# Half rows of the output projection put between the levels of the RWKV inverse

## The reference, cut to what matters

```
z = _rmsnorm(h, mix_pre_g[l]) @ w_in[l]
y_att = _attention_group(z[..., :ATT_IN], cos, sin, attn_out_g[l])
y_rwkv = _rwkv7_group(z[..., ATT_IN:], ...)      # a scan over the tokens, in both directions
mix = jnp.concatenate([y_att, y_rwkv], axis=-1) @ w_out[l]
h = h + _rmsnorm(mix, mix_post_g[l])
f = _swiglu(_rmsnorm(h, ffn2_pre_g[l]), ffn2_w_gate[l], ffn2_w_up[l], ffn2_w_down[l])
```

## Time and profile before

| what | us |
|---|---|
| median of 3 runs | 1143.54 |
| profiled execution | 1142.37 |
| span of the profiled execution | 1140.6 |
| TensorE busy | 1123.6 |
| GpSimd busy | 917.1 |
| ScalarE busy | 633.9 |
| VectorE busy | 542.2 |

### The profile page before, as it was taken

How to read it: one execution, slowest core, us unless ns; L and a number is a source line. 1 busy time by engine, 2 the same in 40 slices (tenths; PEclk the granted TensorE clock), 3 DMA queues, 4 the chain that set the end, 5 groups by cost and what they waited for, 6 DMA issues and landing times.

```text
span 1140.6 us, 24340 instructions
## 1 busy us (share of the span) xinstructions
PE 1123.6 (99%) x10090; PEld 1048.1 (92%) x10090; DVE 542.2 (48%) x1006; ACT 633.9 (56%) x1024; POOL 917.1 (80%) x709
## 2 busy tenths in 40 slices
PE   9999999999999999999999999999999799999998
PEld 9998999999998999999999999999988679999997
DVE  5542575642653223222644333467986466233333
ACT  6666675447644654444744444588664437444443
POOL 6997667875996999989799999698785036999994
PEclk9999999999999999999999999999999999999999
DMA  7655445555565665565556565565610035556563
GB/s 287 194 168 183 129 131 166 204 164 151 185 222 184 211 190 187 189 185 185 166 185 187 186 186 187 193 201 165 199 55 23 4 113 186 186 186 187 188 188 101
DMA packets 54302, 193.50 MB, mean 170 GB/s; under 512 B 6448, under 2 KB 7344, under 8 KB 53808
## 3 DMA queue, kind: packets, MB, share of 16 engines
q1 hardware_dynamic: 52464, 185.41, 51.2%
q10 hardware_dynamic: 1728, 6.53, 1.5%
HBM read 188.77 MB, written 1.05 MB: 166 GB/s over the span
## 4 chain that ended last, share of the span: by engine, by line
PE 95%; DVE 2%; POOL 1%; issue 1%; ACT 1%; DMA 0%; DVEq 0%; POOLq 0%; ACTq 0%
PE product L635 19%; PE product L637 19%; PE product L636 19%; PE bank L765 8%; PE bank L767 7%; PE bank L766 7%; PE product L1382 2%; PE bank L1337 1%; PE bank L1331 1%; PE product L864 1%; PE product L1331 1%; PE product L793 1%; PE product L865 1%; PE product L866 1%; PE bank L822 1%
## 5 line engine op out<-in xcount | busy, mean ns | idle before, releaser
L583 POOL TENSOR_TENSOR weight_lo<-raw_ring,weight_hi 128x512 fp32r<-128x512 f32 x684 | 892.1, 1337 | 191.3 <-ACT weight_hi L2772 177.7
L2772 ACT ACTIVATE weight_hi<-raw_ring 128x1024 fp32r<-128x1024 f32 x338 | 356.7, 1059 | 362.6 <-DMA raw_ring<-in_ffn_gu 108.6
L635 PE MATMUL product<-operand_B_hi,weight_hi 128*128 128x256 f32 x1104 | 312.0, 283 | 0.2 <-POOL weight_lo L583 0.2
L637 PE MATMUL product<-operand_B_hi,weight_lo 128*128 128x256 f32 x1104 | 310.9, 282 | 0.0
L636 PE MATMUL product<-operand_B_lo,weight_hi 128*128 128x256 f32 x1104 | 310.5, 281 | 0.0
L635 PEld LDWEIGHTS product<-operand_B_hi,weight_hi 128*128 128x128 f32 x1104 | 207.8, 188 | 3.3 <-POOL weight_lo L583 0.4
L636 PEld LDWEIGHTS product<-operand_B_lo,weight_hi 128*128 128x128 f32 x1104 | 207.9, 188 | 3.1
L637 PEld LDWEIGHTS product<-operand_B_hi,weight_lo 128*128 128x128 f32 x1104 | 207.8, 188 | 0.0
L635 PE MATMUL product<-operand_A_hi,weight_hi 128*128 128x256 f32 x712 | 203.8, 286 | 0.1
L636 PE MATMUL product<-operand_A_lo,weight_hi 128*128 128x256 f32 x712 | 200.4, 282 | 0.0
L637 PE MATMUL product<-operand_A_hi,weight_lo 128*128 128x256 f32 x712 | 200.4, 281 | 0.0
(11 more groups left out here) (436 smaller groups left out, 1538.6 us busy)
## 6 DMA issues: line engine op xcount, KB each, us to landing
raw_ring<-in_w_in SPq DMA_DIRECT2D x95, 512.0 KB, 3.6
raw_ring<-in_ffn_gu SPq DMA_DIRECT2D x88, 512.0 KB, 3.6
raw_ring<-in_ffn_down SPq DMA_DIRECT2D x44, 512.0 KB, 3.5
raw_ring<-in_w_mlp_up SPq DMA_DIRECT2D x32, 512.0 KB, 3.6
raw_ring<-in_w_mlp_down SPq DMA_DIRECT2D x32, 512.0 KB, 3.5
raw_ring<-in_w_out SPq DMA_DIRECT2D x14, 512.0 KB, 3.7
raw_ring<-in_w_gmlp_v SPq DMA_DIRECT2D x8, 512.0 KB, 3.5
raw_ring<-in_w_branch_c SPq DMA_DIRECT2D x8, 512.0 KB, 3.5
```

Source lines behind the costliest of these rows:

```text
L583: last = k.nc.gpsimd.tensor_tensor(k.wlo[:, slot, part], k.raw[:, slot, part], k.whi[:, slot, part].bitcast(F32), ALU.subtract)
L635: mm(ps, w_hi, op.hi[:, b, :], start=b == 0, stop=False)
L637: return mm(ps, w_lo, op.hi[:, b, :], start=False, stop=b == blocks - 1)
L2772: k.nc.scalar.activation(k.whi[:, slot, 0:w], k.raw[:, slot, 0:w], ACT.Copy).then_inc(k.s["hi_ready"], 1)
```

## The change

All eight pieces of the first token half of tiles 0 to 3 (half rows 0, 2, 4, 6) move between the levels, each behind a group of small products. For that the attention output is made earlier on all engines (`attention_by_feature` stands behind the second level and not the fourth), the banks of the levels of chunks 2 and 3 change so that banks 0 and 1 are free, and `values_first(1)` and `state_behind(1)` become `from_state(1)`. The half rows of the second token half (1, 3, 5, 7) go among the parts of chunk 3, and `last_outputs(3)` goes ahead of `feature_major(0)`. The number of products is the same. The core of the diff:

```diff
-    k.state_banks = (k.slots[1], k.chain_bank, k.slots[1])
-    k.left_banks, k.both_banks = (k.bank[1], k.slots[0]), (k.bank[0], k.bank[3])
+    k.state_banks = (k.chain_bank, k.chain_bank, k.slots[1])
+    k.left_banks = ((k.bank[1], k.slots[0]), (k.slots[1], k.slots[0]))
+    k.both_banks = ((k.bank[0], k.bank[3]), (k.bank[2], k.bank[3]))
-    k.turn_bank = [k.bank[2], k.slots[1]]
+    k.turn_bank = [k.bank[0], k.bank[1]]
...
-        pe.wait_ge(s["op_ready"], k.made["y_mix"].base + AB)
+        pe.wait_ge(s["u_ev"], nth(3, 5))
...
-    pe.wait_ge(s["z_ev"], 10)
-    chunk_products(3, 0, SPARE_BANKS)
+    pe.wait_ge(s["z_ev"], 12)
+    chunk_products(3, 0, LANES[0])
...
         if n == 0:
-            pe.wait_ge(s["tt_ev"], nth(2, 5))
-            pe.wait_ge(s["u_ev"], nth(3, 5))
+            pe.wait_ge(s["op_ready"], k.made["y_mix"].base + AB)
         elif n == 1:
             pe.wait_ge(s["tt_ev"], nth(3, 5))
-            pe.wait_ge(s["op_ready"], k.made["y_mix"].base + AB)
...
     left_and_both(3, 1, 2, 1)
-    pe.wait_ge(s["bc_ev"], 6)
     to_state(0)
     left_and_both(2, 2, 3, 1)
-    values_first(1)
+    attention_by_feature()
     left_and_both(3, 2, 2, 2)
-    state_behind(1)
+    from_state(1)
     left_and_both(2, 3, 3, 2)
     solve(1)
+    half_row(0, slice(0, 1))
     left_and_both(3, 3, 2, 3)
     to_state(1)
+    half_row(0, slice(1, 2))
     left_and_both(2, 4, 3, 3)
-    attention_by_feature()
+    half_row(2, slice(0, 1))
     left_and_both(3, 4, 2, 4)
     from_state(2)
+    half_row(2, slice(1, 2))
     left_and_both(2, 5, 3, 4)
+    half_row(4, slice(0, 1))
     left_and_both(3, 5, 2, 5)
+    half_row(4, slice(1, 2))
     last_both(3)
+    half_row(6, slice(0, 1))
     solve(2)
-    half_row(0)
-    half_row(1)
+    half_row(6, slice(1, 2))
     state_first(2)
     solution_behind(2)
     values_first(3)
-    half_row(2)
+    half_row(1, slice(0, 1))
     state_behind(3)
-    half_row(3)
+    half_row(1, slice(1, 2))
     solve(3)
-    half_row(4, slice(0, 1))
+    half_row(3, slice(0, 1))
+    last_outputs(3)
     feature_major(0)
-    last_outputs(3)
-    half_row(4, slice(1, 2))
-    for n in range(5, 2 * AB):
-        half_row(n)
-
+    half_row(3, slice(1, 2))
+    half_row(5)
+    half_row(7)
     inner_tokens(4)
     inner_tokens(5)
     feature_major(1)
```

More of the change, by code:

```diff
@@ L263 @@
     "v_tok_mm v_tok_ev cb_made cbaq_made y_att_ev y_mixed y_hi aq_mm z_ev nt_in bc_mm bc_ev half_mm "
-    "tt_first u_mm u_ev t_ev tt_mm tt_ev bonus_ev y_taken gains_made nt_turned o_squares "
+    "tt_first u_mm u_ev t_ev tt_mm tt_ev bonus_ev y_taken gains_made nt_turned "
     "x_mm x_ev sa_mm sa_ev yy_mm ss_mm ss_ev y_sq y_sqrt y_norm y_fm y_inner"
@@ L1330, in left_product @@
         n = (k.nf if level in FLIPPED else k.nt)[j % 2]
-        return mm(column(k.left_banks[u // 4], u)[rows], n[rows, u, :], k.tc[j % 2][rows, u, :], start=True, stop=True)
+        return mm(column(k.left_banks[j // 2][u // 4], u)[rows], n[rows, u, :], k.tc[j % 2][rows, u, :], start=True, stop=True)
     def both_product(bank, j, level, u, d):
@@ L1353, in last_both @@
             for d in range(2):
-                last = both_product(k.both_banks[1], j, 5, u, d)
+                last = both_product(k.both_banks[j // 2][1], j, 5, u, d)
         last.then_inc(s["tt_mm"], 2)
@@ L1367, in left_and_both @@
                 for d in range(2):
-                    last_both = both_product(k.both_banks[part], other, at_level, u, d)
+                    last_both = both_product(k.both_banks[j // 2][part], other, at_level, u, d)
             last_left.then_inc(s["u_mm"], 1)
@@ L1411, in values_first @@
         right_of_values, _, outputs_of_values, _ = chunk_parts(j)
-        if j == 1:
-            pe.wait_ge(s["y_taken"], 1)
         for b in range(AB):
@@ L2600, in level_left @@
         four = slice(4 * part, 4 * part + 4)
-        nv.tensor_tensor(k.uc[j % 2][:, four], units(k.left_banks[part])[:, four],
+        nv.tensor_tensor(k.uc[j % 2][:, four], units(k.left_banks[j // 2][part])[:, four],
                          k.levels[:, level:level + 1, :].to_broadcast([P, 4, RC]), ALU.mult).then_inc(s["u_ev"], 1)
@@ L2606, in turned @@
         v.wait_ge(s["tt_mm"], nth(j, level, part))
-        nv.transpose(part_of(flat(k.tc[j % 2]), part), part_of(k.both_banks[part], part)).then_inc(s["t_ev"], 1)
+        nv.transpose(part_of(flat(k.tc[j % 2]), part), part_of(k.both_banks[j // 2][part], part)).then_inc(s["t_ev"], 1)
     def between_levels(j, level, other, at_level):
@@ L2717, in vector_program @@
     first_turned(2)
-    chunk_products(3, 0, SPARE_BANKS)
+    attention_out(7)
+    chunk_products(3, 0, LANES[0])
     left_alone(2, 1)
-    attention_out(7)
+    attention_sums()
     first_turned(3)
@@ L2724, in vector_program @@
         if level == 1:
-            attention_sums()
+            attention_norm()
+        elif level == 2:
+            attention_lows()
         between_levels(2, level + 1, 3, level)
@@ L2728, in vector_program @@
             new_state(0)
-        elif level == 2:
-            attention_norm()
         elif level == 3:
@@ L2743, in vector_program @@
     y_norm(1, 0)
+    rwkv_values(0, 0)
     rwkv_lows(0, 0)
@@ L3339, in inverse @@
             four = slice(4 * part, 4 * part + 4)
-            f(k.ttc[j][:, four], units(k.both_banks[part])[:, four], ACT.Copy).then_inc(s["tt_ev"], 1)
+            f(k.ttc[j][:, four], units(k.both_banks[j // 2][part])[:, four], ACT.Copy).then_inc(s["tt_ev"], 1)
     def last_inverse(j):
         act.wait_ge(s["tt_mm"], nth(j, 5))
-        f(k.ttc[j], units(k.both_banks[1]), ACT.Copy).then_inc(s["tt_ev"], 2)
+        f(k.ttc[j], units(k.both_banks[j // 2][1]), ACT.Copy).then_inc(s["tt_ev"], 2)
     def keys_by_token(j, banks):
@@ L3396, in scalar_program @@
     probabilities(6)
+    f(sm[:, 144:145], k.eps[:, 0:1], ACT.Sqrt)
     probabilities(7)
+    attention_squares()
     right_side(0)
-    keys_by_token(2, (k.bank[2], k.slots[1]))
+    keys_by_token(2, (k.bank[0], k.bank[1]))
     solution(0)
-    attention_squares()
+    attention_root()
     inverse(2, 1)
@@ L3404, in scalar_program @@
     inverse(3, 1)
-    attention_root()
+    attention_highs()
     inverse(2, 2)
@@ L3410, in scalar_program @@
     inverse(2, 3)
+    outputs(1)
     inverse(3, 3)
-    outputs(1)
     inverse(2, 4)
-    attention_highs()
     right_side(2)
```

10 lines of the change are left out of this document (4 added, 6 removed).

## The result

The changed kernel takes 1152.38 us (median of 4 runs, 1150.67 to 1155.19) and the kernel before 1143.67 us (4 runs): 8.7 us slower, ratio 1.0081, 95% interval 1.0058 to 1.0104. The forecast was +4.6 us, with a range up to 1152.0. The profiled execution took 1153.15 us (span 1151.3), 10.8 us more than that of before (1142.37).

What follows compares the result with a forecast made beforehand. TensorE, busy 99% of the span, was taken as the bound: +0.1 us up to the end of solve(2) and +4.5 us behind it make +4.6 us, forecast 1147.6 us, range 1145.0 to 1152.0.

Steps and rivals of the forecast that it cites:

- T: The end of solve(2); tile 0's slot was to be free 9.3 us after it.
- a wait of 6.2 for 6.3: Ahead of solve(3): PE stands 6.3 us for tile 6's load, its ScalarE copy and right_side(3).
- The second wait: Ahead of feature_major(1): PE stands 2.7 us because tile 7's load and copy hold outer_squares and the second norm.
- the whole stretch: End of solve(2) to the turn of the stream: 38.9 us against 34.4 before, so +4.5 us.
- The small gain of 0.3 us in the levels: Up to the end of solve(2): 0.3 us kept of the 1.2 us wait for VectorE's L2552, which goes.
- The rival of the early loads: Tiles 6 and 7: each load takes 3.2 us, not 4.5; total +2.0 us, 1145.0 us; chance 0.12.
- The faster case: Behind solve(2): copies of tiles 6 and 7 hold nothing up; 29.9 us against 34.4, total 1138.5 to 1139; chance 0.06.
- first step: Behind the waits: products keep their earlier durations, such as solve(3) 1.08 us and feature_major(1) to the turn 9.57 us.
- second step: Up to the end of solve(2): seven pieces add 6.9 us and fill 6.5 us of idle time; net +0.1 us.
- its second case: Up to solve(2): pieces do not fill the gaps, each delays its block; total +11.1 us, 1154 us; chance 0.10.
- The gaps themselves: PE's issue gaps among small products, 6.3 us in seven: waits for new instruction blocks, about 252 PE instructions each.

Runs made afterwards that it cites:

- the one with filled waits: Changed kernel plus 24 unread 128x512 products ahead of solve(3) and 12 ahead of feature_major(1); 1150.16 us, ratio 1.0062 against the kernel before.
- the three pieces alone: Change's levels with only three half-row pieces, at the last three places, the others behind solve(2), tiles 0 and 1 freed early; 1141.67 us, ratio 0.9996 against before.
- the shifted kernel: first_left(2)'s 16 products made once more in the kernel before (1144.65 us), or twice more in the changed kernel (1156.69 us), ahead of the levels.

## Why the prediction was wrong

**Right: where the loss arises, and the waits' size.** The chain from tile 0's last product over SP's load and ScalarE's copy to right_side(3) is in the trace step by step: T + 9.1 us for 9.3, a wait of 6.2 for 6.3. The second wait was forecast at 2.7 and is 3.4 us: the load took 0.2 us longer, and outer_squares to the end of the norm 2.6 instead of 2.15 (its last operation on VectorE, ran 1.13 us for 0.69; why is open). With the standing filled, the whole stretch took 39.1 us for 38.9. The small gain of 0.3 us in the levels is borne out too: the wait of 1.2 us for VectorE's L2552 is gone, and one of 0.7 us for its L2595 has come. The direction and the two waits are shown by moving the two copies. The rival of the early loads falls, with 4.6 to 4.7 us a load where it had 3.2. The faster case came about when ScalarE's order was changed, and with only four pieces in the levels and tiles 0 and 1 freed early.

**Wrong, first step: "solve(3) 1.08, piece 0.99, last_outputs 1.31 ..." and "feature_major(1) to the turn, unchanged: 9.57".** These terms have the products behind a wait at the duration that they had in the earlier trace rows, where PE had not stood. After the waits they ran at 1.2 GHz: +2.0 us behind the first, +1.3 behind the second, 3.3 in the profile, and about 2 by the medians (the changed kernel against the one with filled waits, whose intervals overlap). No rival had it. The Trainium skill, "TensorE: Matmul & The Clock Gate", section "HAM oscillation — how this bites in real kernels", describes this very pattern: PE waits for data between two bursts of matmuls and starts the next one at half clock. The trace of the changed kernel agrees, with 1.98 for 1.15 us.

**Wrong, second step: "I take the whole 6.5 us as filled".** The levels were to cost +0.1 us. In the profile they cost +3.3; an estimate from the medians of five kernels with these levels and other ends, less what their profiles show behind solve(2), gives +1.5 to +2.7 (the same sum for the changed kernel itself gives only 0.4, since its profiled run was longer than its median and that of before shorter). The reorder was worth -0.4 to -1.0 (forecast -0.3), so the fault is in the pieces: of their 6.9 us some 2 to 3 by the medians, 2.8 to 4.6 in the profiles, were not filled, which lies between the forecast and its second case. I had put all idle time into one pool. But three of the seven pieces stand behind the last issue gap, in a stretch that had 0.8 us to give, and cost there 2.2 us in the profile of the change and 1.7 in that of the three pieces alone. Two blocks in the middle took in nothing in the profile of the change. How much of a gap a piece takes up in one of the other blocks differs from execution to execution: the six profiles have the same instructions up to solve(2) and take from 40.3 to 42.0 us for the levels. Why is open.

**The gaps themselves** are what the prediction took them for. On the Trainium skill's "mostly hidden" ("Runtime: NRT & Kernel Launch", section "Instruction fetch mechanics"): the shifted kernel shows that the borders are not hidden among the small products, at 0.6 to 1.6 us each.

In the profile the parts add up: forecast 4.6, levels 3.2 more, clock 3.3, the waits and what leads to them 0.4, less the 0.7 of the earlier start, are 10.8 us. By the medians they are estimates: 4.6, and about 2 each for the levels and the clock, come near the 8.7 us.

## What to carry to other kernels

A wait that a change opens ahead of TensorE costs its length and, where PE's clock fell (here with every wait of 2.7 us or more), the slower products behind it: price those at half clock, or look for the cheap cure, which here was the order of one other engine's queue (a copy that nobody needs yet, ahead of one that PE needs). Idle time is filled block by block, not from a pool: list each gap with what is put in front of it, and count pieces that stand behind the last gap in full. Before a product that frees a buffer is moved later, follow the buffer: who loads into it, and which in-order queue stands still until that load has landed.

## What the runs showed of the hardware

- TensorE's clock fell to half in waits of 2.66, 3.37, 5.96 and 6.21 us and 1.4 us behind one of 3.24 us, and did not with one of 1.38 us, nor with the issue gaps of up to 1.6 us. A 128x512 product then took 0.63 instead of 0.39 us in the trace, 32 products of 64x64 1.98 instead of 1.15.
- 36 unread products in place of standing kept the granted clock at 0.999 to 1.0 in all four runs (0.992 to 0.996 without them), and made what is behind solve(2) 3.5 us shorter in the profile, with the first wait ending no sooner.
- Borders of instruction blocks of 256 cost mostly 0.4 to 1.6 us each where PE's instructions are short, and their places follow the count of instructions from the program's start: 64 instructions added earlier shift every later gap to other work.
